# Two transformer blocks on one core: the opening of the first mixer in steps of two channel blocks

## The reference

```python
c_act = jax.nn.silu(c)
mod = c_act @ w_ada[l] + b_ada[l]
sh_m, sc_m, gt_m, sh_f, sc_f, gt_f = jnp.split(mod[:, None, :], N_MOD, axis=-1)
h = rms_norm(x, g_pre_mix[l]) * (1.0 + sc_m) + sh_m
y = token_mixer(h, w_in[l], ...)
x = x + gt_m * rms_norm(y, g_post_mix[l])
```

## Time and profile before

| What | Value |
|---|---|
| Median of three runs | 2620.45 us (2617.8 to 2625.8) |
| Profiled execution, its own time | 2627.55 us |
| Its span | 2625.8 us |
| Busy: TensorE, VectorE, ScalarE, GpSimd | 95%, 66%, 42%, 17% |
| Read from memory | 409.68 MB, 156 GB/s over the span |
| Chain that ended last | TensorE 62%, VectorE 3%, ScalarE 2% |

### The profile page before, as it was taken

How to read it: one execution, slowest core, us unless ns; L and a number is a source line. 1 busy time by engine, 2 the same in 40 slices (tenths; PEclk the granted TensorE clock), 3 DMA queues, 4 the chain that set the end, 5 groups by cost and what they waited for, 6 DMA issues and landing times.

```text
span 2625.8 us, 35204 instructions
## 1 busy us (share of the span) xinstructions
PE 2505.7 (95%) x13498; PEld 2094.4 (80%) x13498; DVE 1724.6 (66%) x2514; ACT 1092.5 (42%) x1876; POOL 446.0 (17%) x462
## 2 busy tenths in 40 slices
PE   4999999999999999999989999999999999999998
PEld 3678987779979878877648888888888888777997
DVE  6967876857995766776865564675565655345454
ACT  3466544556554212236644322324322224334543
POOL 1101111001111111114831112111112110000111
PEclk9999999989999999999989999999999999999999
DMA  8654885536783554542102343442343443221452
GB/s 306 214 176 169 289 290 209 189 135 209 243 279 111 187 176 152 189 157 73 65 16 81 114 175 113 161 176 99 119 178 111 169 168 113 96 74 65 159 197 95
DMA packets 118294, 413.02 MB, mean 157 GB/s; under 512 B 13552, under 2 KB 17776, under 8 KB 118128
## 3 DMA queue, kind: packets, MB, share of 16 engines
q1 hardware_dynamic: 117568, 409.06, 44.6%
q10 hardware_dynamic: 560, 1.72, 0.2%
HBM read 409.68 MB, written 1.05 MB: 156 GB/s over the span
## 4 chain that ended last, share of the span: by engine, by line
PE 62%; DVE 3%; ACT 2%; POOL 1%; issue 1%; DVEq 0%; POOLq 0%; ACTq 0%
PE ps L1102 18%; PE ps L1104 18%; PE ps L1103 18%; PE ps L1318 2%; PE ps L1295 1%; PE ps L1255 1%; PE ps L1286 1%; DVE sl L1673 1%; PE ps L1266 1%; POOL ap L2195 1%; POOL X L2156 1%; ACT F L1440 1%; DVE F L1790 1%; DVE mjunk L1687 0%; ACT sh L1381 0%
## 5 line engine op out<-in xcount | busy, mean ns | idle before, releaser
L1102 PE MATMUL ps<-hH,sh 128*128 128x256 f32 (+1 forms) x2560 | 844.2, 330 | 6.2 <-DVE hL L1761 3.5
L1103 PE MATMUL ps<-hL,sh 128*128 128x256 f32 (+1 forms) x2560 | 837.6, 327 | 0.0
L1104 PE MATMUL ps<-hH,sl 128*128 128x256 f32 (+1 forms) x2560 | 837.6, 327 | 0.0
L1673 DVE TENSOR_TENSOR sl<-raw,sh 128x1024 fp32r<-128x1024 f32 x534 | 655.2, 1251 | 123.4 <-ACT sh L1381 122.7
L1381 ACT ACTIVATE sh<-raw 128x1024 fp32r<-128x1024 f32 x534 | 540.2, 1039 | 394.6 <-PE ps L1104 322.2
L1687 DVE CUSTOM_DVE_ANT_0 mjunk<-raw,cB,V 128x1024 bf16<-128x1024 f32 x384 | 545.5, 1420 | 30.7 <-DMA C<-in_cst 8.4
L1102 PEld LDWEIGHTS ps<-hH,sh 128*128 128x128 f32 x2560 | 481.6, 188 | 58.3 <-issue 7.3
L1103 PEld LDWEIGHTS ps<-hL,sh 128*128 128x128 f32 x2560 | 483.0, 189 | 48.9 <-issue 1.7
L1104 PEld LDWEIGHTS ps<-hH,sl 128*128 128x128 f32 x2560 | 481.6, 188 | 48.3
L2168 POOL TENSOR_TENSOR uLl<-F,uHh 128x256 fp32r<-128x256 f32 (+1 forms) x132 | 166.5, 1261 | 989.9 <-ACT uHh L1562 854.2
L1102 PE MATMUL ps<-sh,uHh 128*128 128x512 f32 x792 | 316.7, 400 | 15.3 <-DVE sl L1673 15.3
(11 more groups left out here) (169 smaller groups left out, 2256.0 us busy)
## 6 DMA issues: line engine op xcount, KB each, us to landing
raw<-in_w SPq DMA_DIRECT2D x756, 512.0 KB, 4.4
raw<-in_w SPq DMA_DIRECT2D x16, 256.0 KB, 3.8
cB<-in_rpb SPq DMA_DIRECT2D x64, 64.0 KB, 2.5
X<-in_x ACTq DMA_DIRECT2D x1, 1024.0 KB, 11.7
X<-in_ctx SPq DMA_DIRECT2D x1, 1024.0 KB, 7.9
out<-X SPq DMA_DIRECT2D x2, 512.0 KB, 2.6
raw<-in_w SPq DMA_DIRECT2D x2, 288.0 KB, 6.1
cB<-in_c ACTq DMA_DIRECT2D x1, 512.0 KB, 5.6
```

The costliest lines, as they stand in the source:

```text
L1102: self.e.matmul(out, lh, rh, start=start, stop=False)
L1103: self.e.matmul(out, lh, rl, start=False, stop=False)
L1104: return self.e.matmul(out, ll, rh, start=False, stop=stop)
L1673: self.e.tensor_tensor(lo[:, 0:w], raw[:, 0:w], hi[:, 0:w].bitcast(F32), ALU.subtract).then_inc(self.sems["w_lo"], 1)
```

## The change

The first layer's opening is rewritten; the second layer keeps its order but for the index scores.

- X is loaded by SP, first in its queue, ahead of V.
- After two sums the squares of both tiles go to ScalarE, then both factors and both scalings, then the scale's first two sums; then `xturn` turns both tiles into `xT` (in the place of O1), and one sum of the next pair is placed.
- `opening` goes through four pairs of channel blocks. For each it places the four sums of the pair (two of shift, two of scale, one of them already placed ahead), makes h for the pair and both tiles (`hpair`), and multiplies it by one unit each of blocks 6, 0 and 1, which fill six banks side by side.
- The other blocks follow in the order 7, 2, 3, 4, 5. The turns of blocks 6, 7, 0 and 1 fall after block 7 and in block 2.
- `index_scores` puts the scores of both tiles (one step a tile) ahead of all ranking, in both layers.
- The rate of the first layer's mixer goes from 0.8 to 1.0 sums a step, that of its second attention from 0 to 0.75. `warm` and the coefficient step of the first mixer are gone.

```diff
@@ -30,7 +30,7 @@
-RATES = {"proj0": 0.8, "proj1": 0.65, "att": 0.0, "out": 0.0, "up0": 0.56, "down0": 0.6, "up1": 0.36, "down1": 0.5,
+RATES = {"proj0": 1.0, "proj1": 0.65, "att0": 0.75, "att1": 0.0, "out": 0.0, "up0": 0.56, "down0": 0.6, "up1": 0.36, "down1": 0.5,
          "ffn2": 1.0, "conv": 0.0, "late": 0.69}
...
@@ -442,31 +442,31 @@
         moba, dsa = stream(0), stream(1)
         self.rate = RATES[f"proj{l}"]
-        def blocks(cb):
+        def blocks(cb, ats=None, banks=None):
             wd, per = (512, 2) if cb < 7 else (72, 8)
-            banks = [self.bank(), self.bank()]
+            banks = banks or [self.bank(), self.bank()]
             return [dict(unit=self.unit(True, [("w_in", l, k, cb * 512, wd) for k in range(at, at + per)]), at=at, per=per,
-                         wd=wd, banks=banks, hid=hid, mid=mid) for at in range(0, KD, per)]
-        begun = {cb: blocks(cb) for cb in (6, 7)}
-        for i in range(2):
+                         wd=wd, banks=banks, act=("h" if l else "h0", hid), mid=mid) for at in ats or range(0, KD, per)]
+        begun = {cb: blocks(cb) for cb in (6, 7)} if l else self.opening(hid, blocks)
+        for i in range(2 if l else 0):
             if i:
                 self.finish_norms()
                 self.warm(4)
-            elif l:
+            else:
                 self.warm(8)
             for cb in (6, 7):
                 for u in begun[cb]:
                     self.add("proj", tiles=[i], last=i == 1, **u)
                     if i:
                         self.pace()
-        for cb in (6, 7, 0, 1, 2, 3, 4, 5):
+        for cb in (6, 7, 0, 1, 2, 3, 4, 5) if l else (6, 0, 7, 1, 2, 3, 4, 5):
             if cb not in begun:
                 begun[cb] = blocks(cb)
                 for u in begun[cb]:
                     at = u["at"]
                     self.add("proj", tiles=[0, 1], last=True, **u)
-                    if at in (2, 4) and pending:
+                    if (at in (2, 4) or not l and cb in (7, 2)) and pending:
                         pending.pop(0)()
                     self.pace()
                     if cb in (3, 4) or (cb, at) in ((2, 4), (2, 6), (5, 0), (5, 2)):
...
@@ -484,6 +484,9 @@
                 def go():
                     turn(("ki",), [20], 1.0, 0)
                     self.index_scores(mid)
+                if not l:
+                    pending.insert(0, go)
+                    continue
             else:
...
@@ -505,7 +508,7 @@
         def take(kp, half):
             return self.unit(True, [w + (k, half * 512, 512) for k in (2 * kp, 2 * kp + 1)])
-        self.rate = RATES["att"]
+        self.rate = RATES[f"att{l}"]
         turn_round(dsa)
         self.pace()
...
+    def opening_mods(self, kp, lo, hi):
+        for u in (2 * kp, 2 * kp + 1, 8 + 2 * kp, 9 + 2 * kp)[lo:hi]:
+            self.jobs.remove(("w_ada", 0, u))
+            self.add("place", unit=self.unit(False, [("w_ada", 0, None, u * 128, D)], ("w_ada", 0, u)))
+    def opening(self, hid, blocks):
+        cbs = (6, 0, 1)
+        banks = {cb: [self.bank(), self.bank()] for cb in cbs}
+        begun = {cb: [] for cb in cbs}
+        for kp in range(4):
+            if kp:
+                self.opening_mods(kp, 1, 4)
+            if 0 < kp < 3:
+                self.opening_mods(kp + 1, 0, 1)
+            self.add("hpair", kp=kp, hid=hid, f=self.next("F", 3))
+            for cb in cbs:
+                u = blocks(cb, (2 * kp,), banks[cb])[0]
+                begun[cb].append(u)
+                self.add("proj", tiles=[0, 1], last=True, **u)
+        return begun
     def index_scores(self, mid):
         def some(i, g2):
...
@@ -546,7 +573,8 @@
         steps = []
         for i in range(2):
-            steps += [lambda i=i: (some(i, 0), some(i, 1)), lambda i=i: (some(i, 2), some(i, 3))]
+            steps += [lambda i=i: [some(i, g2) for g2 in range(4)]]
+        for i in range(2):
             steps += [lambda i=i, lo=lo: self.add("rank", mid=mid, i=i, lo=lo, hi=lo + 2) for lo in range(0, 8, 2)]
         self.turn_at["S"] = -1
...
@@ -843,19 +871,23 @@
         def ab2(l, k, ns):
             return lambda: self.coef("mod_w_2", l, 3 * k, 3 * k + 1, ("norm_g_2", (l, k)), ns)
-        AB = []
         h = self.new()
-        firsts = []
-        self.fill(6)
+        self.opening_mods(0, 0, 2)
+        sts, ys = [], []
         for t in range(2):
-            self.norm_tile(h, t, AB, 0, None, t == 1)
-            firsts.append(self.firsts.pop())
-        self.fill(10)
-        AB.append(ab1(0, 0, "g_pre_mix")())
-        firsts[0]()
-        self.second_parts()
-        self.add("early", upto=len(self.units) + 1)
-        self.firsts += firsts[1:]
+            sts.append(self.rms_open(self.xs(t, 0), D))
+            self.rms_more(sts[t], self.xs(t, 1))
+        for t in range(2):
+            self.rms_close(sts[t], 2)
+            ys.append([self.place("S", j) if t else self.next("PT", 2) for j in range(2)])
+            self.add("scale", t=t, st=sts[t], ys=ys[t], xs=[self.xs(t, 0), self.xs(t, 1)])
+        self.opening_mods(0, 2, 4)
+        for g in range(2):
+            for t in range(2):
+                b = self.bank()
+                self.add("xturn", src=ys[t][g], b=b, k0=4 * g, i=t)
+                self.left(b)
+        self.opening_mods(1, 0, 1)
         h = self.mixer(0, h, ab1(0, 3, "g_pre_ffn"))
         h = self.ffn1(0, h, ab1(1, 0, "g_pre_mix"))
...
@@ -1036,6 +1068,8 @@
                           bias_load=self.bias_load, final=self.final_out)
     def start(self, s):
+        self.e.dma_start(self.m["X"][:, 0:2, :], self.dram["x"].rearrange("b (t p) d -> p (b t) d", p=P)).then_inc(
+            self.sems["ld2"], 16)
         self.e.dma_start(self.m["V"][:, :], self.dram["vec"]).then_inc(self.sems["ld1"], 16)
         self.next = 0
...
                 self.wait_ge(self.got("h", hid, k // 4, t))
+        elif act[0] == "h0":
+            self.wait_ge(self.got("h0", act[1], k // 2))
         elif act[0] == "hc":
...
+    def xturn(self, s):
+        self.wait_ge(self.gone(s["b"]))
+        self.wait_ge(self.got("y", s["src"]))
+        for k in range(4):
+            c = slice(k * 128, (k + 1) * 128)
+            x = self.e.transpose(self.buf(s["b"])[:, c], self.buf(s["src"])[:, c], self.m["C"][:, C_ID:C_ID + 128])
+        x.then_inc(self.sems["tr"], 1)
+        self.done("tr", ("full", s["b"]), ("left", s["src"]))
...
@@ -1359,9 +1404,8 @@
     def start(self, s):
         m, dram = self.m, self.dram
         loads = {0: (m["C"][:, :], dram["cst"]),
-                 2: (m["X"][:, 0:2, :], dram["x"].rearrange("b (t p) d -> p (b t) d", p=P)),
                  4: (m["cB"][:, 0, :], bass.AP(tensor=dram["c"].tensor, offset=0, ap=[[0, P], [1, D]]))}
-        for k in (4, 0, 2):
+        for k in (4, 0):
             self.e.dma_start(*loads[k]).then_inc(self.sems[f"ld{k}"], 16)
         self.wait_ge(self.got("start_ones"))
...
         self.done("a_ps", ("left", p["b"]), ("h_f", p["id"]))
+    def xturn(self, s):
+        self.wait_ge(self.got("full", s["b"]))
+        self.e.copy(self.m["xT"][:, s["k0"]:s["k0"] + 4, s["i"] * 128:(s["i"] + 1) * 128],
+                    cut(self.buf(s["b"])[:, 0:1], [[128, 4], [1, 128]])).then_inc(self.sems["a_ps"], 1)
+        self.done("a_ps", ("left", s["b"]), ("xT", s["k0"] // 4, s["i"]))
+    def hpair(self, s):
+        kp, F = s["kp"], self.buf(s["f"])
+        self.wait_ge(self.gone(s["f"]))
+        self.wait_ge(self.got("A0", kp))
+        self.wait_ge(self.own("a_ps"))
+        self.e.activation(F[:, 0:256], self.m["xT"][:, 2 * kp, :], ACT.Identity, scale=self.m["A"][:, 2 * kp:2 * kp + 1],
+                          bias=self.mcol("w_ada", 0, 0, 0, 2 * kp)).then_inc(self.sems["a_sb"], 1)
+        self.done("a_sb", ("h0_a", kp))
+        self.wait_ge(self.own("a_sb"))
+        self.wait_ge(self.got("h0_v", kp))
+        self.e.activation(self.m["hH"][:, 2 * kp:2 * kp + 2, 0:256], cut(F[:, 0:1], [[256, 2], [1, 256]]),
+                          ACT.Copy).then_inc(self.sems["a_sb"], 1)
+        self.done("a_sb", ("h0_hi", kp))
     def u_free(self, s):
         if s.get("by"):
...
+    def hpair(self, s):
+        kp, F = s["kp"], self.buf(s["f"])
+        for k in (2 * kp, 2 * kp + 1):
+            self.wait_ge(self.got("mod", "w_ada", 0, k, 0))
+            self.wait_ge(self.got("mod", "w_ada", 0, 8 + k, 0))
+        A, B = self.m["A"][:, 2 * kp:2 * kp + 2], self.mcol("w_ada", 0, 0)[:, 2 * kp:2 * kp + 2]
+        self.e.scalar_tensor_tensor(A, self.mcol("w_ada", 0, 1)[:, 2 * kp:2 * kp + 2], 1.0,
+                                    self.vec("g_pre_mix", (0,), 2 * kp, 2), ALU.add, ALU.mult).then_inc(
+            self.sems["v_sb"], 1)
+        self.done("v_sb", ("A0", kp))
+        self.wait_ge(self.own("v_sb"))
+        self.wait_ge(self.gone(s["f"]))
+        for i in range(2):
+            self.wait_ge(self.got("xT", kp // 2, i))
```

(13 more changed lines are left out.)

6 lines of the change are left out of this document (3 added, 3 removed).

## The result

In 20 runs of each kernel in turns the changed one took 2628.43 us (median; 2620.9 to 2635.9) and the kernel before 2624.74 (2617.8 to 2629.2). The ratio is 1.0019, with a 95% interval of 1.0010 to 1.0027: 4 us slower by the medians and 5 by the ratio, inside the 0.3% that I had called "no difference" but outside my range of 2606 to 2624. The profiled execution of the changed kernel took 2625.46 (span 2623.6), 2 us less than that of before; both lie off their medians, in opposite directions.

What follows compares the result with a forecast made beforehand. VectorE's account up to about 167 us was taken to bound the kernel. 17.6 ahead, then 9.7, then 5.7: 2627.55 - 5.7 = 2621.9 for the profiled execution, 2615.0 against the median (chance 0.47); range 2606 to 2624.

Steps and rivals of the forecast that it cites:

- The first product: Opening: TensorE's first product starts at 21.6 us, 18 us earlier than in the kernel before.
- The pair step: Opening: chain of coefficient, VectorE's half, ACT's copy and VectorE's subtraction takes 2.1 us, bounds 1.9 and 3.7.
- The two scalings: Opening: VectorE's scalings of both tiles, behind the squares and factors, end near 13.8 us.
- (d): Opening: X first does nothing for the start, since VectorE's sums bind it; 1.5 us either way, no chance given.
- The landing waits: Opening: two new VectorE waits for weights loaded ahead of four sums but used behind them; 2.6 us, bounds 0 and 6.8.
- From there to the masks' end: Block 2's start to the second masks' end: of 17.6 us won eight are given back, leaving 9.7 ahead.
- The second attention: Second attention and output product: added sums and later lower parts lose 4.0 us, bounds 0 and 9.6, leaving 5.7 ahead.
- A half sum is carried over; 0: Later sums: a half sum carried over costs 0, covered by a feed-forward stage without TensorE gaps.
- The second mixer: Second layer's mixer: reordered index scores change 0 us, bounds 2 either way.
- (a): Second attention: sums fall in VectorE's idle 18 us, so 9.7 to 11 us stays won: 2610; chance 0.30.
- (b): Opening: VectorE's account barely moves, landings cost 6.8 us and pair steps 3.7 each; some 4 us remain: 2619; chance 0.15.
- (c): Opening: TensorE at 1.2 GHz (half clock) makes it slower, 18 us lost and 5.7 won: 2632; chance 0.08.

Runs made afterwards that it cites:

- the kernel with both edits: The changed kernel with owed lower parts ahead of the opening's loads of sums and a look-ahead counting only units with a lower part: 0.9956 against the kernel before.

## Why the prediction was wrong

Its account, step by step, in us ahead of the kernel before.

**The first product: 21.6 forecast, 23.9 measured.** The pair step is right (2.1 forecast, 2.2 measured). The first sum was 1.3 late, since the first weights land at 11.2 and not at 9.9. The two scalings end at 16.1 instead of 13.8, that is 1.0 more: VectorE waits 0.46 and 0.72 for GpSimd's factors. X first was worth 2.9 at this point; rival (d) had it at 1.5 either way.

**The landing waits: 2.6 forecast (bounds 0 and 6.8), 5.8 measured.** The mechanism was the one described (a slot loaded ahead of four sums and freed behind them, loads issued in order); the size was taken too low, with four waits instead of two. The edit that removes it gives 4 us at every landmark up to row 1. These two make 5.5 of the 7.8 us by which block 2 is late (79.85 instead of 72). The rest lies behind the fourth pair: its 36 products take 9.9 us and not 8.2, since the clock falls at 64.0, and the turn 1.6 and not 1.0. So block 2 begins 9.8 ahead and not 17.6.

**From there to the masks' end: 7.9 given back forecast, 8.0 measured** (9.8 to 1.8). VectorE's account of that stretch came out: 78 us forecast from the first index score to the masks' end, 79.6 measured (85.3 to 164.9).

**The second attention: 4.0 lost forecast (bounds 0 and 9.6), 9.8 measured** (1.8 ahead at the masks, 8.0 behind at row 1). This is the step that failed by most. I had named the cause, that the look-ahead counts sums as units, and costed it as four small delays; 9.6 was my bound for no cover at all, and the loss lies just past it. A late lower part costs more than its own microsecond: around TensorE's wait of 2.96 the clock was at 0.5 for 17.1 us and not 10.2, and it fell once more, at 200.5, for 3.4. In the experiment that counts only lower parts all 9.85 come back, 5.5 of it as waiting and 4.3 as slower products. Whether the clock stayed low because of that wait was not tested by itself.

**"A half sum is carried over; 0": a gain of some 0.001 to 0.002 of the time** (3 to 5 us), in the change's favour, and clear of zero only by the edge of its interval (0.9987, up to 0.9999). The same few rows show why no such edit is free: one sum a step earlier meets the context vector's load near 640 and avoids a wait near 1780.

**The second mixer: 0 with bounds of 2, measured 2** from 412 to 580 in one pair of executions, and not by the index order; it is no more than executions differ by.

**The rivals.** (a), the debt hidden in the idle time of the second attention, fell: that time was there, but a sum in it stood ahead of a lower part that TensorE needed. (Its mean clock of 0.86 is one fall of 10.2 us in the 36, not half clock throughout.) (b) had the landings' size right (5.8 of 6.8) and the pair steps wrong. (c), TensorE at 1.2 GHz in the opening, isn't it, though its sign came: the granted clock is 0.5 for 17 us of the opening (23.0 to 29.8, 46.9 to 53.7, 64.0 to 67.4), below the half that it needed, and removing two of the three falls changes neither the start of block 2 (79.80 and 79.85) nor row 1 (0.4) by more than executions differ. The Trainium skill (TensorE: Matmul & The Clock Gate, Part 1: The HAM clock gate) had said that idle gaps bring the slow level back; the trace agrees, with a fall at 46.9 and one at 64.0 around waits of 4.60 and 3.49 us, but the price was paid in the second attention, not here. No rival of mine ended slower through the second attention: its bound of 9.6, with the opening's bounds, would have given it.

Summed with the measured sizes, the opening (7.8 worse) and the second attention (5.8 worse) turn 5.7 ahead into 8.0 behind; less 3 to 5 for the half sum that leaves 3 to 5 us slower, where 4 to 5 were measured. That the two agree so well is in part luck: the 2 us of the second mixer and the 4 to 5 us of the last section are left out of this sum.

## What to carry to other kernels

When work is inserted between the steps of a hand-made order, look at everything that is measured in steps: a look-ahead of "six units" silently becomes four when two of them are of another kind, and a remainder that is carried shifts every later placing. Idle time on an engine hides added work only if it doesn't stand ahead of something that another engine waits for; ask what is queued behind it. Price a late operand by the whole stretch between two landmarks and not by its own wait: here one wait of 2.96 us stood in a stretch that was 9.85 us longer. A change that loses may hold a gain: undoing it part by part found 6 to 12 us in this one.

## What the runs showed of the hardware that I had not expected

**The same stream of products runs at two spacings, with the clock granted in full.** TensorE in windows of the first feed-forward stage, busy all the time (columns: stretch, length, busy and count, granted clock, DMA share, GB/s), in the kernel with both edits and in the one that also has the look-ahead in the second mixer; up to 412 us these two are the same program:

```profile
250.00:270.00 20.00, 20.00 (x179) 1.00 0.85 319
```

```profile
250.00:270.00 20.00, 20.00 (x172) 1.00 0.84 316
```

179 products in 20 us against 172: 0.112 us apart or 0.116, at the same clock of 1.00 and nearly the same DMA traffic. The distances between starts show two values, 0.113 and 0.118, and one or the other holds for tens of microseconds. In the kernel before it was the wider one from 230 us to the end of that stage (172 to 174 in each window that I read), in the changed kernel the closer one (177 to 179); most of the recovery from +9 at 212 to +4 at 412 lies there. A stage of 110 us takes 4 to 5 us more or less by it, as much as the whole effect looked for here. Since the same program showed both, a landmark behind such a stage in one execution is no evidence of a few microseconds, and the gain of the half sum is put down to the repeated runs and the wait at 1781 alone. What chooses the spacing isn't settled; the three kernels without the half sum all began that stage at the wider one, of the eleven with it (the changed one among them) eight had the closer one and three the wider one at 270.

**The same time at half clock went with very different losses.** In the second attention it was 20.5 us instead of 10.2; the same products kept TensorE busy 4.3 us longer, and that stood at row 1. In the opening, waits of 4.60 and 3.49 us went with falls of 6.8 and 3.4 us, again 10.2 together, and without these two falls block 2 began no earlier, since TensorE then waited for another engine.
